# A mixture-of-experts kernel: the scatter of a block's outputs is issued behind the next step's gather of gate and up weights

## What is computed

```python
scores = jax.nn.sigmoid(h @ w_router)                      # 512 tokens, 64 experts
_, idx = lax.top_k(scores + b_router, 8)                   # 8 experts for each token
# the 4096 (token, expert) pairs are sorted by expert and cut into blocks of 128 rows of one expert
def expert_block(acc, blk):
    tok, wt, e = blk
    yb = swiglu(h_pad[tok], w_e_gate[e], w_e_up[e], w_e_down[e]) * wt[:, None]
    return acc.at[tok].add(yb), None                       # scatter with addition
routed, _ = lax.scan(expert_block, zeros, (row_tok, row_w, block_e))
return swiglu(h, w_sh_gate, w_sh_up, w_sh_down) + routed[:n]
```

## Time and profile before

| | us |
|---|---|
| median of 3 runs | 3569.56 |
| lowest and highest run | 3560.85, 3582.76 |
| the profiled execution, as a run | 3566.24 |
| its span, first to last instruction | 3564.4 |

### The profile page before, as it was taken

The page is one execution under the profiler, slowest core; times in us unless marked ns, Lnnn a source line. Parts: engine busy times, 40 slices in busy tenths (PEclk is TensorE's granted clock), DMA queues, the critical chain, the costliest instruction groups (busy, mean ns, idle before and its releaser), DMA issues. The chain is left out here.

```text
span 3564.4 us, 47063 instructions
## 1 busy us (share of the span) xinstructions
PE 3319.5 (93%) x18017; PEld 2823.4 (79%) x18017; DVE 2552.8 (72%) x3696; ACT 1822.4 (51%) x2490; POOL 1115.7 (31%) x665
## 2 busy tenths in 40 slices
PE   7999789799999999995997899999999999899999
PEld 4987568577877878784876677889999998688787
DVE  3453565878988989895344845569988886688786
ACT  3332542578887888886221344333348872233332
POOL 0000300267777787771000000001013334344341
PEclk9999999899999999997998999999999999999999
DMA  5353113477777777785211211236568889999996
GB/s 193 130 173 115 52 54 102 182 255 247 257 251 249 252 244 259 250 269 166 83 59 40 76 36 60 101 133 227 187 232 314 338 334 399 361 377 373 357 369 226
DMA packets 259679, 747.02 MB, mean 210 GB/s; under 512 B 52640, under 2 KB 112816, under 8 KB 225024
## 3 DMA queue, kind: packets, MB, share of 16 engines
q1 hardware_dynamic: 178224, 570.77, 44.2%
q0 software_dynamic: 81232, 173.25, 15.0%
HBM read 793.57 MB, written 110.65 MB: 254 GB/s over the span
## 5 line engine op out<-in xcount | busy, mean ns | idle before, releaser
L2022 DVE TENSOR_TENSOR w_lo<-w_raw,w_hi 128x2048 fp32r<-128x2048 f32 x285 | 652.3, 2289 | 103.5 <-ACT w_hi L1872 99.1
L1872 ACT ACTIVATE w_hi<-w_raw 128x2048 fp32r<-128x2048 f32 x288 | 551.5, 1915 | 29.3 <-DMA w_raw<-in_e_w,over_rows 25.2
L3061 POOL DMA_INDIRECT rows<-in_peer_u_rows,row_at x128 | 177.1, 1384 | 1230.9 <-DVE row_at L3237 805.5
L662 DVE TENSOR_TENSOR w_lo<-w,w_hi 128x1024 fp32r<-128x1024 f32 (+5 forms) x142 | 173.4, 1231 | 279.8 <-ACT w_hi L636 278.8
L1530 PE MATMUL ps_peer<-peer_xT_hi,w_hi 128*128 128x384 f32 x1024 | 352.8, 345 | 13.6 <-DVE w_lo L3152 13.5
L3152 DVE TENSOR_TENSOR w_lo<-w_raw,w_hi 128x2048 fp32r<-128x2048 f32 x128 | 293.0, 2289 | 98.5 <-ACT w_hi L3072 97.9
L2214 PE MATMUL ps_gu<-w_hi,h2T_hi 128*128 128x512 f32 x792 | 321.6, 406 | 26.7 <-DVE w_lo L2022 24.2
L1532 PE MATMUL ps_peer<-peer_xT_hi,w_lo 128*128 128x384 f32 x1024 | 343.5, 335 | 0.0
L1531 PE MATMUL ps_peer<-peer_xT_lo,w_hi 128*128 128x384 f32 x1024 | 343.5, 335 | 0.0
L636 ACT ACTIVATE w_hi<-w 128x1024 fp32r<-128x1024 f32 (+5 forms) x142 | 149.7, 1063 | 350.2 <-DMA w<-in_w_in 228.3
L1530 PE MATMUL ps_peer<-w_hi,coef_hi 128*128 128x512 f32 x768 | 301.6, 393 | 24.6 <-DVE w_lo L3152 22.5
(11 more groups left out here) (546 smaller groups left out, 8281.6 us busy)
## 6 DMA issues: line engine op xcount, KB each, us to landing
w_raw<-in_e_w SPq DMA_DIRECT2D x195, 1024.0 KB, 6.4
w_raw<-in_peer_u SPq DMA_DIRECT2D x64, 1024.0 KB, 6.0
w_raw<-in_peer_v SPq DMA_DIRECT2D x64, 1024.0 KB, 9.2
w<-in_w_in SPq DMA_DIRECT2D x60, 512.0 KB, 4.8
acts<-act_out SPq DMA_DIRECT2D x64, 384.0 KB, 6.6
gates<-gate_tile SPq DMA_DIRECT2D x6, 4096.0 KB, 17.1
gates_back<-gates SPq DMA_DIRECT2D x16, 1536.0 KB, 15.4
act_back<-acts SPq DMA_DIRECT2D x64, 384.0 KB, 10.7
```

Source lines behind the costliest of these rows:

```text
L1872: nc.scalar.activation(w_hi[:, slot(n), :], w_raw[:, slot(n), :], ACT.Copy).then_inc(hi_done.sem, 1)
L2022: nc.vector.tensor_tensor(w_lo[:, slot(n), :], w_raw[:, slot(n), :], w_hi[:, slot(n), :].bitcast(F32), ALU.subtract).then_inc(lo_done.sem, 1)
L3061: nc.gpsimd.indirect_dma_start(out=row(i), out_offset=None, in_=src, in_offset=bass.IndirectOffsetOnAxis(ap=row_at[:, which, k:k + 1], axi ...
```

## The change

In POOL's loop, `put` moves one step later and to another place in it. Before, step b ended with put(b), and step b + 1 began with the gate and up gathers that become possible at that step. Now step b + 1 begins with these gathers, and put(b) comes behind them, ahead of `take_weights` and `take_rows`. The last put comes behind the loop.

```diff
@@ -1852,6 +1852,8 @@
                 for n in refills:
                     if freed(n) == b and units[before(n)][1] < 2:
                         over_weights(n)
+                if b > T:
+                    put(b - 1)
                 if b >= T + 1 and b + 3 < NB:
                     pool.wait_ge(out_done.sem, 2 * b)
                     take_weights(b + 3)
@@ -1861,7 +1863,7 @@
                 for n in refills:
                     if freed(n) == b and units[before(n)][1] == 2:
                         over_weights(n)
-                put(b)
+            put(NB - 1)
             for s in range(NO):
                 pool.wait_ge(stored[s].sem, 16 * len(range(s, NB, NO)))
```

## The result

The changed kernel is slower: 3607.35 us, the median of 4 runs (3602.99 to 3609.12), against 3571.2 of the kernel before on the same chip (3560.85 to 3582.76). The ratio is 1.0116, with a 95% interval of 1.0092 to 1.0139. The profiled execution took 3608.37 us with a span of 3606.6; before, 3566.24 and 3564.4.

The account below looks back on a forecast made before the run. PE sets the pace at 9.307 us a step, with POOL's twelve places full. The sum 3566.2 - 33.7 + 84 = 3616.5, about 3620 against the median, was taken as 3618 us; range for 8 in 10: 3550 to 3675.

Parts of the forecast that it names:

- (1): Up gathers of over blocks, issued ahead of the put, come early; all six PE stalls go, -33.7 us.
- (2): On POOL, the gate gather's wait now holds the put behind it: put(7) late by 4.5 us, put(8) by 5.5.
- (3): put(9) waits for put(8) to land, starts just inside a `low`; the down gather goes out 8 us later.
- (4): ACT gets the over block's down unit 3.5 us late, between 1.3 and 5.6; whole price 5.6 us a stall.
- the six of before: Six PE stalls in the kernel before, up gathers directly behind a put: 5.6 us each, of which 3.9 idle.
- (5): Every second cycle stalls: 15 stalls, none to 30 as bounds, 15 x 5.6 = 84 us.
- hold or fail by a hair: put(8) lands shortly before 794.8 and out(10) is due at about 794.3; no cost of its own counted.
- few new stalls: Rival: a stall sets POOL back to an early phase; 6 to 9 stalls, 3570 to 3586 us, chance 0.25.
- the gate gathers' wait for `ps_gu`: Sign for the later puts: on POOL, gate gathers show a wait for the gate and up products; no size given.
- the 9.4 named: Sign for the late down gathers: PE's transposes are over 9.4 us apart on average, 9.68 before.
- all stalls go: Rival: nothing comes back if put(9) starts under 8.0 us after put(8) ends; 3536 us, 0.9% faster, chance 0.15.
- Every cycle stalls: Rival: POOL and the scatters become the bound outright; 30 stalls, 3704 us, or 3641 with idle only, chance 0.10.

Follow-up runs that it names:

- after: The changed kernel, gathers ahead of the put, against the kernel before: 3607.35 us, ratio 1.0116.
- the one-input `low`: Changed kernel with `low` on DVE as a one-element reduction reading one SBUF tensor, not a two-input subtraction; low parts left out of the result: 3527.12 us.
- `low` in halves: Each `low` written as two 128x1024 instructions, same computation: changed kernel 3530.33 us, kernel before 3523.87 us.
- the third buffer: Changed kernel with three block_out buffers instead of two, so out(b) waits for the scatter of b - 3: 3612.36 us.
- the order made from the places: New POOL loop order with three output buffers: put(b - 2) first in step b, next the down gather, then gate or up: 3594.42 us.

## Why the prediction was right

Forecast 3618 us, slower by over 1%; measured 3607.35. Each step of it against the runs:

**(1) The gain of 33.7 us** was there in full: no up or gate unit of an over block is waited for, and the kernel with the other half of the change alone, where the up gather stays behind the put, waits for it in practically every cycle (28 of 30).

**(2) and (3) The puts.** By hand: put(7) from 775.5, put(8) from 784.8, put(9) from 794.8 to 798.2, the down gather from 803.45. The trace has 775.41, 784.71, 794.72 to 798.16 and 803.33. All lie within 0.15 us, and ran as two rules had them: an indirect DMA ends 0.9 us (a put 1.5) behind the `low` in which it begins, and the next scatter can start some 8.4 us after a late one ended. The second rule is the prediction's 8.4 us "after the issue": the rows give 8.4 from the end of that put and 10.0 from its start, and the prediction added it to an end, rightly. It was right for this cycle (786.32 to 794.72), but it is no constant: in the order with puts two steps behind it failed.

**(4) The late down gather** cost ACT 4.31 us at block 12, forecast 3.5 within 1.3 to 5.6. The price of 5.6 us a stall, taken over from the six of before, fits the mean of the nine (50.4 / 9), each of which leaves PE idle for 4.0 us in the mean and not 3.5; singly they cost 3.7 to 7.5.

**(5) How often.** This term was mis-sized. Forecast 15 x 5.6 = 84 us; the stage lost 74.4: 50.4 in nine late down gathers, 21.4 in nine waits of `out`, 2.6 in steps longer by 0.2 to 0.3. I had seen out(b + 2) hold or fail by a hair and let it "add to the same stalls". In fact it made stalls of its own, in other cycles, at 2.4 us. Where it fails by 2 us it delays PE just enough that the down gather behind it is only 0.4 us late. At blocks 43, 46, 49, 52 and 55 it does so cycle after cycle. So there are 18 stalls and not 15, at 4.0 us in the mean. Put into the sum: 3566.2 - 33.7 + 74.4 = 3606.9, and the profiled execution took 3608.4. That the total came so close to 3618 is in part luck. Of the kind of stall that the forecast counted and priced there are nine, not 12 to 20, and with these alone the sum is 3566.2 - 33.7 + 50.4 = 3582.9, inside the range of "few new stalls". The 21.4 us of `out`, which the forecast put at nothing of their own, made up most of the 33.6 us that were missing (84 - 50.4), and carried the result over 1%.

Of the signs that the prediction named, the gate gathers' wait for `ps_gu` was the weak one: 25.3 us in 8 waits only, since POOL mostly came to them late. The steps are 10.1 us apart (912.0 / 90), above the 9.4 named.

The rival "all stalls go" is refuted as a forecast. Its condition was that put(9), and its like in each cycle, starts under 8.0 us after the end of the put before. In after it does so in 10 of 29 cycles (median 8.4 us); with the one-input `low` in 27 of 29 (median 5.5), and there the new order loses nothing. But the condition is not needed: with `low` in halves it holds in 6 of 29 only, and no stall of over 2.2 us is left, since POOL then has time behind a late put. Its other source, that `tensor_tensor` does not hold POOL, is refuted by the one-input run. (The prediction calls it "the second rival" once; it stands first.) "Few new stalls" had the number of the late down gathers (nine) but not the waits of `out`. "Every cycle stalls" did not come, by my reading because stalls give places back; what speaks for it is the 1.24 us of the gathers issued during a stall, and the third buffer, which took the waits of `out` away and had as much time come back as late gathers.

What stays open: why a scatter takes 3 to over 10 us from its end to its landing (2.9 to 10.6 in the kernel before), and why longer in the order made from the places.

## What to carry to other kernels

Before an order on one queue is changed, ask why its instructions take as long as they do: here a DVE instruction with two SBUF inputs held the indirect DMAs that began inside it, and writing it in two took away all but 0.5 and 6.8 us of what the two orders lost, while the reordering only moved the stalls. Where a queue has no spare place, an instruction moved ahead pushes all behind it into places that may not exist, and a stall removed (a third buffer) comes back elsewhere, dearer. A wait that holds "by a hair" deserves a term of its own.

## What was not expected of the hardware

An indirect DMA gets in between two instructions of DVE that follow each other without a gap, so the hold is that of one instruction: 1.22 us in place of 2.29, at 0.16 us more of DVE's time. And the landing of an accumulating scatter moves with the order around it, 7.8 us from issue in the median before and 10.2 in the order made from the places, although it is the same scatter of the same rows.
